# A table of expert rows laid out by rounds of 32, and its block loads moved from ScalarE's queue to SyncE's

## The reference, cut to what matters

```python
best = jnp.argmax(group_score, axis=-1)
in_group = jnp.arange(N_GROUPS) == best[..., None]
masked = jnp.where(in_group[..., None], sel, -jnp.inf).reshape(scores.shape)
_, idx = lax.top_k(masked, TOP_K)
w = jnp.take_along_axis(scores, idx, axis=-1)
w = w / jnp.sum(w, axis=-1, keepdims=True)
...
a = jnp.einsum('bld,edf->blef', h, w_gate)
u = jnp.einsum('bld,edf->blef', h, w_up)
return jnp.einsum('blef,efd->bld', jax.nn.silu(a) * u * gates[..., None], w_down)
```

## Time and profile before

| | |
|---|---|
| runs | 1338.50, 1336.86, 1333.83 us; median 1336.86 us |
| the profiled execution | 1333.37 us, its span 1331.4 us |
| TensorE matmuls | 951.5 us busy, 71% of the span |
| VectorE, ScalarE, GpSimd | 28%, 22%, 4% |
| bytes moved | 256.86 MB, 193 GB/s on average |
| TensorE's granted clock | 0.837 of full speed on average |
| experts of layer 0 | from 528 to 794 us of the span |
| experts of layer 1 | from 1059 to 1305 us |

### The profile page before, as it was taken

The page is one execution under the profiler, slowest core; times in us unless marked ns, Lnnn a source line. Parts: engine busy times, 40 slices in busy tenths (PEclk is TensorE's granted clock), DMA queues, the critical chain, the costliest instruction groups (busy, mean ns, idle before and its releaser), DMA issues.

```text
span 1331.4 us, 13746 instructions
## 1 busy us (share of the span) xinstructions
PE 951.5 (71%) x5481; PEld 488.7 (37%) x5481; DVE 374.3 (28%) x908; ACT 297.1 (22%) x690; POOL 49.6 (4%) x62
## 2 busy tenths in 40 slices
PE   5999887877668984385828715998998438591971
PEld 2456555653444542121203203554454212130321
DVE  0331065763455013010101005346622301010112
ACT  2320232243346013010101004116731201010111
POOL 0300000000000001000000000000001100000001
PEclk8899988887889996597868956996999659796895
DMA  9999965255540222457667842040003245675724
GB/s 396 423 419 412 414 264 194 93 188 210 183 146 1 94 96 95 167 223 234 256 222 283 353 169 85 0 169 29 1 7 136 102 164 222 237 279 198 291 103 158
DMA packets 35089, 256.86 MB, mean 193 GB/s; under 512 B 2800, under 2 KB 2944, under 8 KB 20048
## 3 DMA queue, kind: packets, MB, share of 16 engines
q1 hardware_dynamic: 16848, 185.68, 36.9%
q0 software_dynamic: 11696, 44.91, 8.6%
q10 hardware_dynamic: 6480, 25.36, 4.9%
HBM read 203.17 MB, written 52.77 MB: 192 GB/s over the span
## 4 chain that ended last, share of the span: by engine, by line
PE 50%; DMA 27%; DVE 12%; ACT 5%; issue 3%; POOL 1%; ACTq 0%; POOLq 0%; SPq 0%; DVEq 0%
DMA expert_rows<-U 21%; PE ps L456 17%; PE ps L568 8%; PE ps L805 5%; DMA U<-expert_rows 4%; PE ps L590 3%; PE ps L470 2%; PE ps L420 2%; PE ps L552 2%; DMA ring<-w_in 1%; PE ps L495 1%; PE ps L724 1%; DVE U L1529 1%; PE ps L477 1%; PE ps L516 1%
## 5 line engine op out<-in xcount | busy, mean ns | idle before, releaser
L568 PE MATMUL ps<-ring,U 128*32 128x512 f32 x1200 | 176.8, 614 | 56.1 <-DVE U L1395 56.1
L568 PE MATMUL ps<-hT,U 128*32 128x512 f32 x168 | 81.3, 642 | 37.0 <-DVE U L1395 37.0
L456 PE MATMUL ps<-U,ring 128*128 128x384 f32 x320 | 105.1, 487 | 2.7 <-DVE U L1309 1.4
L568 PEld LDWEIGHTS ps<-ring,U 128*32 128x32 f32 x1200 | 47.2, 114 | 149.3 <-issue 91.3
L590 PE MATMUL ps<-ring,U 128*32 128x512 f32 x672 | 93.5, 634 | 10.1 <-ACT U L970 10.1
L1395 DVE COPY U<-ps 128x512 f32<-128x512 f32 x24 | 16.6, 691 | 266.8 <-DMA expert_rows<-U 216.7
L552 PE MATMUL ps<-small,U 128*128 128x128 f32 x192 | 32.0, 318 | 74.7 <-DMA U<-expert_rows 72.6
L568 PE MATMUL ps<-U 128*32 128x512 f32 x168 | 81.3, 642 | 0.0
L456 PEld LDWEIGHTS ps<-U,ring 128*128 128x128 f32 x320 | 60.1, 189 | 47.4 <-issue 4.2
L970 ACT COPY U<-ps 128x512 f32<-128x512 f32 x24 | 14.1, 585 | 256.4 <-DMA expert_rows<-U 221.9
L805 PE MATMUL ps<-ring,hT 128*128 128x384 f32 x192 | 65.9, 503 | 5.7 <-ACT hT L883 4.9
(11 more groups left out here) (246 smaller groups left out, 1311.2 us busy)
## 6 DMA issues: line engine op xcount, KB each, us to landing
ring<-w_in SPq DMA_DIRECT2D x102, 1536.0 KB, 11.1
expert_rows<-U POOLq DMA_DIRECT2D x15, 2048.0 KB, 75.0
U<-expert_rows ACTq DMA_DIRECT2D x24, 512.0 KB
expert_rows<-U ACTq DMA_DIRECT2D x24, 512.0 KB
hT<-w_in SPq DMA_DIRECT2D x6, 1536.0 KB, 8.5
U<-w_in SPq DMA_DIRECT2D x6, 1536.0 KB, 13.2
small<-small_in SPq DMA_DIRECT2D x1, 3147.5 KB, 34.5
xT<-x_in SPq DMA_DIRECT2D x1, 1536.0 KB, 16.7
```

The source lines that it names most:

```text
L456: ins = mm(out, lhs(k), rhs(k), start=(k == 0), stop=(k == n - 1))
L568: ins = mm(ps[q:q + 32, r, :], xgT[:, r, P * k + q:P * k + q + 32], w[e][:, c:c + 512], start=(k == 0), stop=(k == DC - 1))
```

## The change

`CAP` goes from 480 to 512, and the table's order changes: first the round of 32 rows, then the expert, then the row in the round. Round r of expert e lies at row 512 r + 32 e, so that block i, the rows of four neighbouring experts in one round, is one run of 128 rows. VectorE computes the row number from 512 e + s (s: the token's place in its expert) with one more copy, three tensor-scalar and two tensor-tensor operations on integers of 128 x 6, the last of which takes the place of the old copy. The clear has 16 DMAs in place of 15. All block loads leave ScalarE: SyncE issues them in threes, the first three after the wait for `scattered` and ahead of the layer's ninth slot, the three of group g ahead of slot 8g + 2 of the layer and behind that slot's wait for its buffer. ScalarE's queue has the stores alone.

```diff
-CAP = 480
+CAP = 512
...
+        key_i, key_e, key_r = (rt[:, 792 + 6 * i:798 + 6 * i].bitcast(mybir.dt.int32) for i in range(3))
...
-        block_of = lambda rows, i: rows.rearrange("(e s) n -> e s n", e=NE)[GS * (i // NR):GS * (i // NR) + GS, 32 * (i % NR):32 * (i % NR) + 32, :]
-        by_expert = lambda tile: tile
-        beyond_rows = lambda rows, e, b: rows[bass.ds(e * CAP + (NR * 32 + P * b), P), :]
+        block_of = lambda rows, i: rows[32 * NE * (i % NR) + P * (i // NR):32 * NE * (i % NR) + P * (i // NR) + P, :]
+        beyond_rows = lambda rows, e, b: rows.rearrange("(r q) n -> r q n", q=32 * NE)[NR + 4 * b:NR + 4 * b + 4, bass.ds(e * 32, 32), :]
...
+            def rows_in(l, g):
+                for r in range(NR):
+                    i = NR * g + r
+                    if g:
+                        sp.wait_ge(S["turned1"], N_BLOCK * l + i - NR + 1)
+                    sp.dma_start(xgb[r], block_of(rows_d, i)).then_inc(xg_full[r], 16)
+
             for n in range(N_SLOTS):
                 if RELEASED[n]:
                     sp.wait_ge(S["slot_used"], RELEASED[n])
-                if n in (S_MOE0 + 2 * GS, S_MOE1 + 2 * GS):
-                    sp.wait_ge(S["scattered"], 32 * NT * (2 if n > S_MOE1 else 1))
+                for l, first in enumerate((S_MOE0, S_MOE1)):
+                    if n == first + 2 * GS:
+                        sp.wait_ge(S["scattered"], 32 * NT * (l + 1))
+                        rows_in(l, 0)
+                    for g in range(1, NG):
+                        if n == first + 2 * GS * g + 2:
+                            rows_in(l, g)
                 sp.dma_start(buffers[IN_BUFFER[n]], w_d[row_of_slot(n), :, :]).then_inc(slot_full[IN_BUFFER[n]], 16)
...
-                act.wait_ge(S["scattered"], 32 * NT * (l + 1))
-
-                def load(i):
-                    if i >= N_BLOCK:
-                        return
-                    if i >= NR:
-                        act.wait_ge(S["turned1"], n0 + i - NR + 1)
-                    act.dma_start(by_expert(xgb[i % NR]), block_of(rows_d, i)).then_inc(xg_full[i % NR], 16)
...
                     act.copy(xgT[:, i % NR, 0:512], ps[:, 3, :]).then_inc(S["xgT_act"], 1)
-                    load(i + NR)
...
-                    act.dma_start(block_of(rows_d, i), by_expert(ysb[i % 2])).then_inc(y_stored[i % 2], 16)
-
-                for r in range(NR):
-                    load(r)
+                    act.dma_start(block_of(rows_d, i), ysb[i % 2]).then_inc(y_stored[i % 2], 16)
+
...
-                dve.tensor_copy(row_of, row_f).then_inc(S["rows_ready"], 1)
+                link(dve.tensor_copy(key_i, row_f))
+                ts(key_e, key_i, 9, 5, ALU.logical_shift_right, ALU.logical_shift_left)
+                ts(key_r, key_i, 480, 4, ALU.bitwise_and, ALU.logical_shift_left)
+                link(ts(key_i, key_i, 31, None, ALU.bitwise_and))
+                link(tt(key_e, key_e, key_r, ALU.bitwise_or))
+                tt(row_of, key_e, key_i, ALU.bitwise_or).then_inc(S["rows_ready"], 1)
```

## The result

| | before | after |
|---|---|---|
| median | 1335.34 us (4 runs) | 1156.32 us (4 runs, 1152.52 to 1165.88) |
| ratio | | 0.8666, interval 0.8616 to 0.8716 |
| profiled execution | 1333.37 us | 1165.88 us, its span 1163.0 us |
| TensorE's granted clock | 0.837 | 0.892 |

The forecast was 1155 us with a range of 1138 to 1200. The profiled execution is the slowest of those measured, some 10 us above the median, and part of what makes it so can be seen in it. In one experiment, *Loads earlier*, the profiled execution (1175.15 us at a granted clock of 0.883) counts as slow, and the ratio is that of its three fellows.

A forecast was written before the change was run, and what follows sets the result against it. Blocks on four of 16 DMA engines were taken to bound the groups. The changed stretch, 2 x (153.9 + 5) + 3 + 1.7 = 322.5 us for 504.8, saves 182.3 off the 1336.86 us median: forecast 1155 us, range 1138 to 1200.

The forecast's parts named there:

- The bound and its cause: Experts: blocks keep four of 16 DMA engines busy, in agreement with their access pattern's outermost size of 4.
- the 60.8 us budget: Old group period: six blocks 30.5 us on four engines plus eight weight slots 30.3 us, against 64.8 us store to store.
- The sum: Scatter landing to last store landing, both layers, plus row numbers: 322.5 us in place of 504.8, 182.3 us less.
- scatter to `up(0)`: First loads on SyncE: `up(0)` starts 10.0 us behind the scatter, against 28.9 us before.
- waits for blocks: Between groups: late loads of blocks 6 and 9 stall TensorE 1.2 and 2.2 us; 5 us per layer taken.
- The end of layer 0: Last store shares engines with the next layer's weights, slots 38 and 39: 3 us, bounds 0 and 6.
- the clear: First 170 us: a sixteenth DMA adds 2.1 MB, 5 us of saturated queue; cost zero, at most 5 us.
- the rows' order: Path to the scatter: six small row-number operations in place of one, 0.87 us, two layers 1.7 us.
- The store step: Stores alone on ScalarE's queue: 6.6 us for block 0's store before `rows_out(2)`; bound 1 us per group, within the 5.
- The rate that sets the groups: Rival: mixed row stores and weight reads make groups go at DMA's pace; 1187 us at 350 GB/s, 1229 at 300; chance 0.24.
- It does not do what it says: Rival: 4 KB rows, not four engines, give 103 GB/s; 1335 us or up to 20 more; no effect, chance 0.05.
- fewer engines: Rival listed among the forecast's chances at 0.03; its description is not in the text given.

The follow-up runs named there:

- Loads earlier: Changed kernel with the block loads of groups 2 and 3 issued half a group earlier, ahead of slots 14 and 22 of the layer: 1164.08 us, ratio 0.8695.
- the kernels with two and with four DMAs: Kernel before, old table, each block load and store cut into two DMAs of two experts each: 1538.5 us; into four, one per expert: 1204.27 us.

## Why the prediction was right

**The bound and its cause** held. The four engines, 5.08 us a block and the 60.8 us budget were right, and the kernels with two and with four DMAs show that the cause goes with the outermost size, which the trace of before could only suggest. Where the pieces lie apart, size 2 had a share of 0.13, size 4 one of 0.25, and four DMAs of 32 rows reached 1.00. Where they are one run, 128 rows reached 1.08, 8 x 16 reached 1.07 and 4 x 32 reached 1.00. Why the share goes with this size, and which engines they are, no trace here shows.

**The sum** asked for 2 x 158.9 + 3 = 320.8 us in the changed stretch, and 322.7 were measured. Two misses offset each other in it: layer 0 took 166.1 us where 161.9 were forecast, layer 1 156.6 where it was 158.9. Its terms, by layer 0's chain: scatter to `up(0)` 9.4 us (10.0 forecast); `up(0)` 20.7 (21.6); waits for blocks 612.86 - 610.2 = 2.6 and 649.8 - 648.4 = 1.4 us (1.2 and 2.2 forecast, 5 per layer taken). In layer 1 from the start of `up(3)` to the last landing 1136.62 - 1100.13 = 36.5 us, which is 20.64 + 11.8 + 0.75 + 3.3 to the tenth. Only the pace of the groups was another than the sum took. From `up(1)` to `up(2)` and on to `up(3)` layer 0 has 38.2 and 36.9 us and layer 1 39.3 and 36.3, not TensorE's 35.5: the mean is close to the 37.5 us that a group's bytes take at 419 GB/s. So DMA set the pace, for 4.2 us in layer 0 and 4.6 in layer 1 beyond TensorE's, within the 5 that the sum allowed. `up(3)` started 120.1 us after the scatter landed, with 117 forecast.

**Two terms were mis-sized.** The end of layer 0 was put at 3 us more than layer 1's, at most 6; it is 710.70 - 664.71 = 46.0 against 36.5, so 9.5 us. The forecast had slots 38 and 39 sharing with one store. In fact four more slots, issued at 680.2 us in the sixth step of `up(3)`, still moved, two stores in a row stood in the chain, and each took three times its time. And the clear, "zero, at most 5; the scatter at 521 us is the cover", failed as a step: its cover was not the scatter but VectorE's state part at 181 us, which reuses the source of the clears. I had asked who reads the table, not who needs the buffer that the clear reads. It cost 8.5 us in the profiled execution, above the bound of 5, and the granted clock fell with it, 0.74 in the stretch from 180 to 200 us where before had 1.00. Of the 12.7 us by which the scatter landed later, the row numbers below are 0.75; about 3 us I can't assign.

**That the median came out within 2 us** is in part luck: the profiled execution, for which the sum gave 1151, took 1165.9, the other runs less. Nor did the sum know how much the start differs from execution to execution: layer 0's scatter landed 11 us apart in six profiles of kernels with the same 16 clears. For the rows' order 0.87 us per layer was forecast; the old copy took 0.17 us, and now it is 531.98 to 532.90, so 0.75 us more. The first and the last of the six operations:

```profile
531.98 0.17 DVE L1367 CAST U<-U 128x6 int32<-128x6 f32 x1
532.73 0.17 DVE L1372 TENSOR_TENSOR U<-U 128x6 int32<-128x6 int32 x1
```

**The store step** was right in its effect only. I gave a store 6.6 us of slack and forecast the waits nearly gone; the median landing is 9.5 us, and L973 still waits 53.5 us in total and L1401 40.4. It is hidden, since TensorE asks for that copy only in the sixth step of the next `up`.

**The rivals.** The rate that sets the groups fell in its numbers, 300 to 350 GB/s: they were my assumption, between the 276 and the 431 of the earlier trace rows, and with everything in flight it was 419. But its mechanism was near, since the groups did go at DMA's pace at that rate. "It does not do what it says" fell with the share of a lone block, 1.08, and so did the chance of 0.03 for fewer engines.

## What to carry to other kernels

Read the DMA share of a stretch where one kind of transfer runs alone: 0.25 is as much as four of 16 engines, and then look at the outermost size of its pattern and at whether its pieces adjoin, not at its bytes: the same 512 KB a block had shares of 0.13, 0.25 and 1.08 here. Blocks at a share of 0.25 held up both queues in which they were tried, with stores of 45.7 and 46.0 us in the chain on ScalarE's and loads of 27 to 42 us on SyncE's, so mend the shape before moving a transfer between queues. And for work called hidden, list who waits for its buffers as well as who waits for its result: the clear's buffer cost 8.5 us.

## What I had not expected of the hardware

With blocks of share 0.25, or cut into DMAs of 32 rows, in flight beside weights, there were stretches in which the DMA engines were fully busy at 276 to 322 GB/s (276 and 286 in the earlier trace rows, 322 with four DMAs), though others ran at 431 and, with four DMAs at 600 to 604 us, at 426; with blocks of 128 rows beside the same weights it was 419 for 88 us. So a full share was not always a full rate here. What holds these engines then was not tried.
